# Layer 0's modulation: shift and scale ahead by fp32 products, the other 32 column tiles inside the attention

## The chip, the cores and the metric

The kernel runs on one core of a Trainium2 chip. The metric is the device time of one execution in microseconds (us). Three runs of the kernel before gave 3951.24, 3951.5 and 3957.62 us; the median is 3951.5.

## What is computed

One inference step of a diffusion backbone of four layers. Two groups of tokens run through it, 512 latent tokens and 128 context tokens, each token 1024 wide. Layers 0 and 3 mix tokens by latent attention with 16 heads, layer 1 by an RWKV-7 scan in both directions, layer 2 by pooling; behind each mixer stands a SwiGLU feed-forward block. Each layer gets six vectors per group out of the conditioning, and they steer both its halves:

```
def adaln(cond, w, b):
    m = (jax.nn.silu(cond) @ w + b)[..., None, :]
    return jnp.split(m, 6, axis=-1)

def modulate(x, shift, scale):
    return x * (1.0 + scale) + shift
...
        mp = adaln(c_ctx, ada_w[layer], ada_b[layer])
        ms = adaln(c, ada_w[layer], ada_b[layer])
        hp = modulate(yp, mp[0], mp[1])
        hs = modulate(ys, ms[0], ms[1])
...
        yp = layer_norm(ALPHA * yp + mp[2] * op, ln_g[layer, 0], ln_b[layer, 0])
        ys = layer_norm(ALPHA * ys + ms[2] * os_, ln_g[layer, 0], ln_b[layer, 0])
        fp = swiglu(modulate(yp, mp[3], mp[4]), ffn_wg[layer], ffn_wu[layer], ffn_wd[layer])
```

`ada_w` of a layer is 1024 x 6144 in fp32, 24 MB. The mixer's input needs only the first two of the six vectors (shift and scale, 2048 columns); the gate comes into play behind the mixer's output projection, the last three in the feed-forward block.

## The kernel before

Activations lie transposed in SBUF: `x` is 128 partitions x 8 tiles x 640 tokens. Most products are made three times in fp32r on a high and a low part of both operands (`w_hi`, `w_lo`, `hhi`, `hlo`). The weights come as a stream of 512 KB chunks of eight 128x128 tiles: SP loads them into three raw buffers (`w_raw`), POOL splits them into high and low, and TensorE (PE) takes them in the order of the stream. `panel` (L807, its products at L819) makes one output tile of 128x640 out of eight tiles.

The order of work on each engine is that of the code; the engines meet at semaphores, and at the ends of some stages (`end`) all three of PE, ACT and DVE wait for each other.

**The opening.** SP issues the constants, x (2560 KB) and then layer 0's `ada_w` in 24 units of 1 MB (128 partitions x 4 row tiles x 512 columns) into a ring of four slots. `ada` on ACT (L1523) casts each unit to its high part, on DVE (L2112) subtracts for the low part, and on PE (L825) multiplies: the conditioning (two columns, `silu_hi` and `silu_lo`) is the stationary operand, 512 columns of the unit move (L837). The results are rows of 2x512; ACT copies them out (L1534), and 48 small fp32 products with the identity turn them into columns (L842: two moving columns, a 2x128 stationary operand). DVE copies all 48 tiles out, adds the bias and prepares the combined scales of the layer (`modulation`, L2123). Then ACT modulates x tile by tile and casts (`split_h`, L1546, operations at L1560 and L1552), DVE subtracts (L2169), and PE starts its first panel.

**The attention of layer 0** (`mla`, PE L981, ACT L1617, DVE L2339). Behind the projections eight pairs of heads run in a loop, which PE has unrolled four times. A pair begins with two key panels (L1046) and six query tiles (L819), and then takes ten steps `u`, five blocks of 128 queries for each head. In a step PE makes the scores of block u+1 (`scores`: four fp32 passes of 320 columns at L1067, or two of 128 at L1064 for the context block), turns the exponentials of block u (`turn`: five transposes at L1077) and multiplies those of block u-1 with the values (`av`: five fp32 products of 64 columns, ten passes, at L1091). DVE takes the maximum (L2390), copies the turned tile out (L2413, L2414) and scales the result (`tail`, L2382); ACT makes the exponential (L1682). At a pair's end PE turns the output (L1105). An fp32 product is two passes through PE, so it has two MATMUL and two LDWEIGHTS rows in the trace. After the eighth pair comes the output projection (`out_proj`), whose results DVE multiplies with the gate and adds to x (`gated`, L2181).

Of the kernel before, what the change touches and what calls it, by code (L numbers as in the profile page):

```python
# [49 lines left out]
ADA_SLOTS, ADA_SPLITS = 4, 3  # L50
# [169 lines left out]
def build(nc, a, o):  # L220
    ctx = ExitStack()
    with ctx:
# [19 lines left out]
        sc_hi, sc_lo = sb("silu_hi", [P, KD, 2], F32R), sb("silu_lo", [P, KD, 2], F32R)  # L242
# [28 lines left out]
        stage_free = sem("stage_free")  # L271
        s_init, s_const = sem("s_init"), sem("s_const")
        ada_land = [sem(f"ada_land{i}") for i in range(ADA_SLOTS)]
        unit_land = [sem(f"unit_land{i}") for i in range(2)]
        unit_used, unit_sum, unit_col = sem("unit_used"), sem("unit_sum"), sem("unit_col")
        ada_mm, ada_row, ada_hi, ada_lo = sem("ada_mm"), sem("ada_row"), sem("ada_hi"), sem("ada_lo")
# [12 lines left out]
        def f_ada(m, g):  # L289
            m.rows = g("ada_rows", [2, 6 * D])  # L290
            m.hi, m.lo = ([g(f"ada_{n}{i}", [P, 4, 512], F32R) for i in range(ADA_SPLITS)] for n in ("hi", "lo"))
            m.ring = [g(f"ada_ring{i}", [P, 4, 512]) for i in range(ADA_SLOTS)]
# [19 lines left out]
        def f_mla(L):  # L312
            def f(m, g):
# [20 lines left out]
                m.mx = g(f"m_mx{L}", [P, 2])  # L334
            return f
# [144 lines left out]
        def _(sp):  # L480
            sp.dma_start(cst[:, :], a["cst"]).then_inc(s_const, 16)
            sp.dma_start(x[:, :, :], a["x"].rearrange("k p t -> p k t")).then_inc(s_const, 16)
            done = 0
# [318 lines left out]
        def _(pe):  # L802
# [22 lines left out]
            def ada():  # L825

                m = m_ada
                for cb in range(12):
                    if cb >= 2:
                        pe.wait_ge(ada_row, cb - 1)  # L830
                    for kh in range(2):
                        unit = 2 * cb + kh
                        pe.wait_ge(ada_lo, unit + 1)
                        hi, lo = m.hi[unit % ADA_SPLITS], m.lo[unit % ADA_SPLITS]
                        for n, (w, r) in enumerate(((sc_hi, hi), (sc_lo, hi), (sc_hi, lo))):
                            for k in range(4):
                                last = mm(ps[0:2, 4 + cb % 2, :], w[:, 4 * kh + k, :], r[:, k, :],  # L837
                                          start=kh == 0 and n == 0 and k == 0, stop=kh == 1 and n == 2 and k == 3)
                        last.then_inc(ada_mm, 1)
                pe.wait_ge(ada_row, 12)  # L840
                for n in range(48):
                    mm(ps[:, 6, 2 * n:2 * n + 2], m.rows[0:2, n * P:(n + 1) * P], ident[0:2, 0:2], start=True, stop=True)  # L842
                end()
                end()
# [136 lines left out]
            def mla(L):  # L981
# [526 lines left out]
            pe.wait_ge(s_const, 32)  # L1508
            end()
# [8 lines left out]
        def _(act):  # L1518
# [3 lines left out]

            def ada():  # L1523
                m = m_ada
                for u in range(ADA_UNITS + 3):
                    if u < ADA_UNITS:
                        act.wait_ge(ada_land[u % ADA_SLOTS], 16 * (u // ADA_SLOTS + 1))
                        if u >= ADA_SPLITS:
                            act.wait_ge(ada_mm, u - ADA_SPLITS + 1)
                        nc.scalar.copy(m.hi[u % ADA_SPLITS][:, :, :], m.ring[u % ADA_SLOTS][:, :, :]).then_inc(ada_hi, 1)  # L1530
                    if u >= 4 and u % 2 == 0:
                        cb = u // 2 - 2
                        act.wait_ge(ada_mm, 2 * cb + 2)
                        nc.scalar.copy(m.rows[0:2, cb * 512:(cb + 1) * 512], ps[0:2, 4 + cb % 2, :]).then_inc(ada_row, 1)  # L1534
                end()
                end()
# [80 lines left out]
            def mla(L):  # L1617
# [5 lines left out]
                else:  # L1623
                    split_h(2 * L, x, lambda kt, cd: (mods[0][:, KD + kt, cd:cd + 1], mods[0][:, kt, cd:cd + 1]), m.t32, m.hhi)
# [47 lines left out]
                end()  # L1672
                with act.Fori(0, HEADS // 2) as j:
# [416 lines left out]
            act.wait_ge(s_const, 32)  # L2090
            act.wait_ge(s_init, 2)
            ch(af(sc_c[:, :, :], cond, ACT.Silu))
            nc.scalar.copy(sc_hi[:, :, :], sc_c[:, :, :]).then_inc(s_init, 1)
            end()
            for L in range(DEPTH):
                if L == 0:
                    ada()
# [9 lines left out]
        def _(dve):  # L2107
# [4 lines left out]
            def ada():  # L2112
                m = m_ada
                for u in range(ADA_UNITS):
                    dve.wait_ge(ada_hi, u + 1)
                    tt(m.lo[u % ADA_SPLITS][:, :, :], m.ring[u % ADA_SLOTS][:, :, :], m.hi[u % ADA_SPLITS][:, :, :].bitcast(F32),
                       ALU.subtract).then_inc(ada_lo, 1)
                end()
                ch(cp(mods[0][:, :, :], ps[:, 6, 0:96].rearrange("p (n c) -> p n c", c=2)))
                modulation(0)  # L2120
                end()

            def modulation(L):  # L2123

                mod = mods[L % 2]
                ch(tt(mod[:, :, :], mod[:, :, :], adab[:, L, :].unsqueeze(2).to_broadcast([P, 48, 2]), ALU.add))
                for part in (1, 4):
# [211 lines left out]
            def mla(L):  # L2339
# [28 lines left out]
                with dve.Fori(0, HEADS // 2) as j:  # L2368
# [31 lines left out]
                    copy_pt(dve, q, m, j, 9)  # L2400
                    tail(9)
# [4 lines left out]
                end()  # L2406
                out_proj(L, mods[L % 2][:, 2 * KD:3 * KD, :])
# [372 lines left out]
            nc.vector.memset(eps[:, 3:5], 0.0).then_inc(s_init, 1)  # L2780
            dve.wait_ge(s_const, 32)
            dve.wait_ge(s_init, 3)
            ch(tt(sc_lo[:, :, :], sc_c[:, :, :], sc_hi[:, :, :].bitcast(F32), ALU.subtract))
            end()
# [202 lines left out]
```

## Time and profile before

| | |
|---|---|
| runs of the kernel | 3951.24, 3951.5, 3957.62 us |
| span of the profiled execution | 3955.7 us (its whole time is not listed apart) |
| PE busy | 3625.6 us (92%) |
| PE weight load busy | 3412.5 us (86%) |
| DVE busy | 2466.1 us (62%) |
| ACT busy | 938.1 us (24%) |
| POOL busy | 1840.3 us (47%) |
| chain that ended last | PE 71%, DVE 16% of the span |

The span goes from the first to the last instruction of one profiled execution on the chip. PE is the matmul side of TensorE and PEld its weight loads, which overlap; ends of matmuls are modelled. Busy shares are averages over stages that have different limits. The granted clock is the share of 2.4 GHz that TensorE was given: 1.00 is 2.4 GHz, 0.50 is 1.2 GHz. Where a row ends in brackets, they hold the idle time of the engine before it and what ended that.

### The profile page before, as it was taken

The page shows a single profiled execution, that of the slowest core. Times are in us where ns is not written, and L with a number is a line of the kernel's source. Part 1 is how long each engine was busy: PE and PEld are TensorE (multiplying, and loading weights), DVE is VectorE, ACT ScalarE, POOL GpSimd, SP SyncE. Part 2 cuts the span into 40 slices and gives each one's busy share as a digit, 9 for nine tenths or more (in the row PEclk, how much of TensorE's full clock was granted, in tenths as well). Part 3 has the DMA queues.
Part 4 walks back from the last instruction along what each step waited for, and adds up shares of the span by engine and source line. Part 5 has one row for each costly group of instructions (what it writes and reads, how often), then busy time and mean ns, then how long its engine had stood idle before and what let it go on. Part 6 is the DMA issues. An engine that isn't in the chain of part 4 may idle for free.

```text
span 3955.7 us, 74569 instructions
## 1 busy us (share of the span) xinstructions
PE 3625.6 (92%) x31532; PEld 3412.5 (86%) x31532; DVE 2466.1 (62%) x3517; ACT 938.1 (24%) x1804; POOL 1840.3 (47%) x875
## 2 busy tenths in 40 slices
PE   8999999999889778888999994899999989999998
PEld 3877799999788678888999994799998777899997
DVE  5366678758785466655885768886676566632125
ACT  5322231001244255532310012310013222220011
POOL 1311156665455646535566552466554101356663
PEclk9999999999999888889999997899999999999999
DMA  8200024333235543322343331243332000122221
GB/s 318 62 12 17 17 81 147 136 112 123 70 127 182 149 87 94 84 55 102 114 142 119 124 101 36 90 145 128 123 102 73 27 12 17 43 70 75 76 76 53
DMA packets 226844, 367.60 MB, mean 93 GB/s; under 512 B 104752, under 2 KB 111088, under 8 KB 226416
## 3 DMA queue, kind: packets, MB, share of 16 engines
q1 hardware_dynamic: 171408, 255.08, 20.9%
q10 hardware_dynamic: 55136, 107.98, 7.9%
q8 instruction: 254, 4.16, 0.4%
q14 instruction: 46, 0.38, 0.0%
HBM read 326.47 MB, written 36.54 MB: 92 GB/s over the span
## 4 chain that ended last, share of the span: by engine, by line
PE 71%; DVE 16%; issue 3%; ACT 3%; DMA 1%; SPq 1%; POOL 1%; ACTq 1%; DVEq 0%; POOLq 0%
PE ps L819 52%; PE ps L1091 3%; PE ps L1067 3%; DVE f_acc L2159 2%; PE ps L862 2%; PE ps L1077 2%; DVE m_mx L2390 1%; PE ps L1046 1%; DVE r_t L2456 1%; DVE x L2257 1%; DVE r_hlo L2440 1%; DVE ps L2605 1%; PE ps L1027 1%; DVE x L2266 1%; PE ps L879 1%
## 5 line engine op out<-in xcount | busy, mean ns | idle before, releaser
L674 POOL TENSOR_TENSOR w_hi<-w_raw,zrow 128x1024 fp32r<-128x1024 f32 x354 | 693.7, 1959 | 1783.6 <-PE ps L819 979.9
L676 POOL TENSOR_TENSOR w_lo<-w_raw,w_hi 128x1024 fp32r<-128x1024 f32 x354 | 900.2, 2543 | 27.8
L2159 DVE SCALAR_TENSOR_TENSOR f_acc<-f_unit,silu_c,f_acc 128x512 f32<-128x512 f32 x504 | 631.3, 1293 | 7.6
L819 PE MATMUL ps<-f_hhi,w_hi 128*128 128x320 f32 x2688 | 634.1, 317 | 0.0
L819 PE MATMUL ps<-f_hhi,w_lo 128*128 128x320 f32 x2688 | 613.0, 309 | 0.0
L819 PE MATMUL ps<-f_hlo,w_hi 128*128 128x320 f32 x2688 | 610.8, 308 | 0.0
L819 PEld LDWEIGHTS ps<-f_hlo,w_hi 128*128 128x128 f32 x2688 | 449.6, 188 | 0.0
L819 PEld LDWEIGHTS ps<-f_hhi,w_lo 128*128 128x128 f32 x2688 | 448.9, 188 | 0.0
L819 PEld LDWEIGHTS ps<-f_hhi,w_hi 128*128 128x128 f32 x2688 | 441.2, 188 | 0.0
L819 PE MATMUL ps<-f_ahi,w_hi 128*128 128x320 f32 x1408 | 322.2, 310 | 0.2 <-DVE f_alo L2304 0.2
L819 PE MATMUL ps<-f_alo,w_hi 128*128 128x320 f32 x1408 | 320.9, 309 | 0.0
L819 PE MATMUL ps<-f_ahi,w_lo 128*128 128x320 f32 x1408 | 320.6, 309 | 0.0
L2302 DVE TENSOR_TENSOR f_a<-f_sil,ps 128x640 f32<-128x640 f32 x88 | 72.2, 821 | 376.0 <-ACT f_sil L1603 376.0
L2181 DVE SCALAR_TENSOR_TENSOR x<-ps,mod,x 128x320 f32<-128x320 f32 (+2 forms) x264 | 99.7, 433 | 331.6 <-PE ps L819 330.4
L2304 DVE TENSOR_TENSOR f_alo<-f_a,f_ahi 128x640 fp32r<-128x640 f32 x88 | 201.7, 2293 | 69.9 <-ACT f_ahi L1605 69.9
L819 PEld LDWEIGHTS ps<-f_ahi,w_hi 128*128 128x128 f32 x1408 | 235.6, 188 | 1.1 <-DVE f_alo L2304 0.5
L819 PEld LDWEIGHTS ps<-f_ahi,w_lo 128*128 128x128 f32 x1408 | 235.5, 188 | 0.0
L819 PEld LDWEIGHTS ps<-f_alo,w_hi 128*128 128x128 f32 x1408 | 235.2, 188 | 0.0
L1603 ACT ACTIVATE f_sil<-ps 128x640 f32<-128x640 f32 x88 | 62.3, 708 | 711.7 <-DVE f_acc L2159 383.2
L1091 PE MATMUL ps<-m_V,m_PT 128*128 x1344 | 170.4, 271 | 15.5 <-DVE m_PT L2416 11.7
L1091 PEld LDWEIGHTS ps<-m_V,m_PT 128*128 128x128 f32 x1344 | 162.5, 192 | 22.2 <-issue 20.2
L1682 ACT ACTIVATE m_P<-ps,m_nm 128x640 f32<-128x640 f32 x128 | 101.6, 793 | 332.6 <-DVE m_nm L2394 332.6
(401 smaller groups left out, 6710.4 us busy)
## 6 DMA issues: line engine op xcount, KB each, us to landing
w_raw<-in_w SPq DMA_DIRECT2D x340, 512.0 KB, 3.5
f_unit<-in_ada_w ACTq DMA_DIRECT2D x72, 1024.0 KB, 5.8
ada_ring<-in_ada_w SPq DMA_DIRECT2D x24, 1024.0 KB, 6.6
up_scratch<-r_o ACTq DMA_DIRECT2D x40, 320.0 KB, 3.3
s_LW<-up_scratch SPq DMA_DIRECT2D x16, 320.0 KB, 5.1
s_LA<-up_scratch SPq DMA_DIRECT2D x8, 640.0 KB, 6.6
x<-in_x SPq DMA_DIRECT2D x1, 2560.0 KB, 9.4
x_scratch<-r_o ACTq DMA_DIRECT2D x8, 320.0 KB, 2.2
```

The source lines that it names most:

```text
L674: nc.gpsimd.tensor_tensor(whi[:, slot, :], raw[:, raw_slot, :], zrow[:, 0:1].to_broadcast([P, CH * P]), ALU.add).then_inc(w_hi_done, 1)
L676: nc.gpsimd.tensor_tensor(wlo[:, slot, :], raw[:, raw_slot, :], whi[:, slot, :].bitcast(F32), ALU.subtract).then_inc(w_split, 1)
L819: last = mm(ps[:, 2 * b + h, 0:HT], w, r[:, h * HT:(h + 1) * HT], start=kt == 0 and n < 2, stop=kt == KT - 1 and n >= 4)
L862: last = mm(ps[:, 2 * b + h, 0:HT], w, r[:, h * HT:(h + 1) * HT], start=kt == 0 and n == 0, stop=kt == KT - 1 and n == 2)
L1067: last = mm(ps[:, b + h, 0:HT], m.Q[:, hh, qt * P:(qt + 1) * P], m.K[:, hh, h * HT:(h + 1) * HT], start=True, stop=True)
L1077: last = nc.tensor.transpose(ps[:, 4 + kb // 4, (kb % 4) * P:(kb % 4 + 1) * P], m.pr[:, u % 2, kb * P:(kb + 1) * P], ident)
L1091: last = mm(ps[:, 6, 0:64], m.pt[:, u % 2, kb * P:(kb + 1) * P], m.V[:, kt, bass.ds(j * P + hh * 64, 64)], start=kb == 0, stop=kb == nk - 1)
L1682: af(halves(m.pr[:, u % 2, :]), ps[:, b:b + 2, 0:HT], ACT.Exp, bias=m.nm[:, 2 * (u % 2), 0:1], scale=SM_SCALE, accum_out=m.nm[:, 2 * (u % ...
L2159: last = stt(acc[:, cd, :], unit[:, k, :], by, acc[:, cd, :], ALU.mult, ALU.add)
L2181: last = stt(xs, ps[:, 2 * b + h, t0:t1], gate[:, c, cd:cd + 1], xs, ALU.mult, ALU.add)
L2302: tt(halves(m.a32[:, f % 2, :]), halves(m.sil[:, f % 2, :]), pair(2 * b + 1), ALU.mult).then_inc(q.act, 1)
L2304: tt(m.alo[:, u, :], m.a32[:, f % 2, :], m.ahi[:, u, :].bitcast(F32), ALU.subtract).then_inc(q.lo, 1)
```

## The change

Layer 0's 48 column tiles of modulation are computed in two parts, both on PE in fp32 without a split: a 128x128 tile of `ada_w` is the stationary operand, and the two columns of the conditioning move. A tile takes eight such products and comes out as a column.

- Ahead: the first 16 tiles (shift and scale), out of 8 units in 8 buffers, without a ring. DVE adds the bias out of PSUM and 1 to the scale. ACT's casts, DVE's subtractions, the rows and the turning products are gone, as are three of the common stage ends.
- Inside the attention: the other 32 tiles, four to each pair of heads, in steps u = 1, 3, 6 and 8, between `scores` and `turn` on PE. Each tile is a load of its own (128 partitions x 8 x 128, 512 KB in pieces of 512 bytes) that ACT issues: three at the start of a pair, the fourth in step 3, when the first has been used. DVE copies four tiles out of PSUM at the end of each pair. The rest of `modulation` follows after the attention.
- On SP x is loaded behind the units and the first chunk of weights; the silu waits for the constants alone.

```diff
-ADA_SLOTS, ADA_SPLITS = 4, 3
+EARLY = 2 * KD // 4
+LATE_AT = 2 * KD
+LATE_GROUPS = 4
+LATE_BUFFER = (0, 1, 2, 0)
+LATE_TURN, LATE_AV = (1, 3, 6, 8), ()
...
-            sp.dma_start(x[:, :, :], a["x"].rearrange("k p t -> p k t")).then_inc(s_const, 16)
...
-            for u in range(ADA_UNITS):
-                slot = u % ADA_SLOTS
-                if u >= ADA_SLOTS:
-                    sp.wait_ge(ada_lo, u - ADA_SLOTS + 1)
-                sp.dma_start(m_ada.ring[slot][:, :, :],
+            for u in range(2 * EARLY):
+                sp.dma_start(m_ada.unit[u][:, :, :],
                              src[:, 4 * (u % 2):4 * (u % 2) + 4, (u // 2) * 512:(u // 2 + 1) * 512]
-                             ).then_inc(ada_land[slot], 16)
+                             ).then_inc(ada_land[u // 2], 16)
...
-                    pieces(LAYER_BASE[L], [[(c, 0, CH)] for c in MLA_IN])
+                    order = [[(c, 0, CH)] for c in MLA_IN]
+                    pieces(LAYER_BASE[L], order, 0, 1)
+                    if L == 0:
+                        sp.dma_start(x[:, :, :], a["x"].rearrange("k p t -> p k t")).then_inc(s_x, 16)
+                    pieces(LAYER_BASE[L], order, 1)
...
+                pe.wait_ge(s_cond, 1)
+                for cb in range(EARLY):
+                    units = m_ada.unit[2 * cb:2 * cb + 2]
+                    pe.wait_ge(ada_land[cb], 32)
+                    for n in range(4):
+                        for k in range(KD):
+                            last = mm(ps[:, 6, 8 * cb + 2 * n:8 * cb + 2 * n + 2], units[k // 4][:, k % 4, n * P:(n + 1) * P],
+                                      sc_c[:, k, :], start=k == 0, stop=k == KD - 1)
+                last.then_inc(ada_mm, 1)
+
+            def late(j, p):
+
+                b = LATE_BUFFER[p]
+                pe.wait_ge(ada_land[b], j * 32 + 16 * (p // 3 + 3) if b == 0 else j * 16 + 48)
+                for k in range(KD):
+                    last = mm(ps[:, 7, 2 * p:2 * p + 2], m_mla[0].late[b][:, k, :], sc_c[:, k, :], start=k == 0, stop=k == KD - 1)
+                last.then_inc(late_mm, 1)
...
                         if u < 9:
                             scores(u + 1)
+                        if L == 0 and u in LATE_TURN:
+                            late(j, LATE_TURN.index(u))
                         if u < 10:
                             turn(u)
+                        if L == 0 and u in LATE_AV:
+                            late(j, len(LATE_TURN) + LATE_AV.index(u))
                         if u:
                             av(u - 1)
...
                 else:
+                    act.wait_ge(s_x, 16)
+                    act.wait_ge(ada_mod, 1)
                     split_h(2 * L, x, lambda kt, cd: (mods[0][:, KD + kt, cd:cd + 1], mods[0][:, kt, cd:cd + 1]), m.t32, m.hhi)
...
                 with act.Fori(0, HEADS // 2) as j:
+                    if L == 0:
+                        for p in (0, 1, 2):
+                            load_late(j, p)
                     for u in range(10):
                         qt = u % 5
+                        if L == 0 and u == LATE_TURN[0] + 2:
+                            act.wait_ge(late_mm, j * LATE_GROUPS + 1)
+                            load_late(j, 3)
                         act.wait_ge(q.nmax, q.at.nmax + j * 10 + (u + 1))
...
+                dve.wait_ge(ada_mm, 1)
+                mod = mods[0]
+                ch(tt(mod[:, 0:LATE_AT, :], ps[:, 6, 0:2 * LATE_AT].rearrange("p (n c) -> p n c", c=2),
+                      adab[:, 0, 0:LATE_AT].unsqueeze(2).to_broadcast([P, LATE_AT, 2]), ALU.add))
+                s = mod[:, KD:2 * KD, :]
+                ts(s, s, 1.0, None, ALU.add).then_inc(ada_mod, 1)
...
                     copy_pt(dve, q, m, j, 9)
+                    if L == 0:
+                        dve.wait_ge(late_mm, j * LATE_GROUPS + LATE_GROUPS)
+                        cp(mods[0][:, bass.ds(j * LATE_GROUPS + LATE_AT, LATE_GROUPS), :],
+                           ps[:, 7, 0:2 * LATE_GROUPS].rearrange("p (n c) -> p n c", c=2))
                     tail(9)
...
                 end()
+                if L == 0:
+                    modulation(0)
                 out_proj(L, mods[L % 2][:, 2 * KD:3 * KD, :])
```

On PE the program of before opens with 72 such rows of wide products (three to a unit, the first five here), then the 48 turning products, then the first panel (x4 counts equal products in a row; `m_hhi` is the split x):

```order
L837 MATMUL ps<-ada_hi,silu_hi 2x512 x4
L837 MATMUL ps<-ada_hi,silu_lo 2x512 x4
L837 MATMUL ps<-ada_lo,silu_hi 2x512 x4
L837 MATMUL ps<-ada_hi,silu_hi 2x512 x4
L837 MATMUL ps<-ada_hi,silu_lo 2x512 x4
```

With the change it opens like this (`ada_unit` is the tile of `ada_w`, `silu_c` the conditioning, and L821 the panel's line):

```order
L835 MATMUL ps<-silu_c,ada_unit 128x2 x128
L821 MATMUL ps<-m_hhi,w_hi 128x320 x2
L821 MATMUL ps<-m_hhi,w_lo 128x320 x2
L821 MATMUL ps<-m_hlo,w_hi 128x320 x2
```

All products of 512 columns are gone, and what is left ahead of the first panel is one row of 128 products with two columns.

On SP the queue of before opens so:

```order
L481 DMA cst<-in_cst 128x844
L482 DMA x<-in_x 128x8x640
L648 DMA ada_ring<-in_ada_w 128x4x512 x24
L511 DMA w_raw<-in_w 128x1024 x6
```

and now so:

```order
L484 DMA cst<-in_cst 128x844
L646 DMA ada_unit<-in_ada_w 128x4x512 x8
L512 DMA w_raw<-in_w 128x1024
L659 DMA x<-in_x 128x8x640
L512 DMA w_raw<-in_w 128x1024 x5
```

x has moved behind the units and a chunk of weights, and 16 of the 24 units have left the queue.

In the attention PE's program of before reads so from the value products of step 2 on (`m_K` and `m_Q` make the scores, `cst` and `m_P` the transposes, `m_V` and `m_PT` the value products):

```order
L1091 MATMUL ps<-m_V,m_PT 128x64 x5
L1064 MATMUL ps<-m_K,m_Q 128x128
L1073 REGISTER_ALU
L1077 MATMUL ps<-cst,m_P 128x128 x5
L1091 MATMUL ps<-m_V,m_PT 128x64 x5
L1067 MATMUL ps<-m_K,m_Q 128x320 x2
```

and with the change:

```order
L1092 MATMUL ps<-m_V,m_PT 128x64 x5
L1065 MATMUL ps<-m_K,m_Q 128x128
L842 ISA
L844 MATMUL ps<-silu_c,m_late 128x2 x8
L1074 REGISTER_ALU
L1078 MATMUL ps<-cst,m_P 128x128 x5
L1092 MATMUL ps<-m_V,m_PT 128x64 x5
L1068 MATMUL ps<-m_K,m_Q 128x320 x2
```

A wait (L842) for the tile's load and its eight products have come between the scores and the transposes; the same stands in steps 1, 6 and 8.

## Rows read from the trace of the kernel before

**Rows 1.** The page's slices: granted clock and DMA, 40 equal slices.
```profile
PEclk9999999999999888889999997899999999999999
DMA  8200024333235543322343331243332000122221
```

**Rows 2.** Order of time, opening: start us, length us, engine, line, [idle before <- releaser].
```profile
1.20 0.42 SPq L482 DMA_DIRECT2D x<-in_x  x1
...
10.66 0.22 ACT L2092 ACTIVATE silu_c<-cst 128x16 f32<-128x16 f32 x1 [8.33 <-DMA x<-in_x]
...
13.43 1.90 ACT L1530 CAST ada_hi<-ada_ring 128x2048 fp32r<-128x2048 f32 x1 [2.31 <-DMA ada_ring<-in_ada_w]
...
16.07 1.90 ACT L1530 CAST ada_hi<-ada_ring 128x2048 fp32r<-128x2048 f32 x1 [0.75 <-DMA ada_ring<-in_ada_w]
```

**Rows 3.** The chain that ended last, around the first split: start us, us, what.
```profile
106.89 0.27 DVE mod L2126
...
107.39 0.18 DVE mod L2129
...
108.24 1.21 ACT m_t L1560 x2
...
124.12 22.27 PE ps L819 x150
```

**Rows 4.** Order of time, PE in the first pair of heads and its end.
```profile
184.71 0.61 PE L1046 MATMUL ps<-m_khi,w_hi 128*128 128x384 f32 x2 [1.01 <-ACTq L473]
...
197.84 1.23 PE L1091 MATMUL ps<-m_V,m_PT 128*128 x10
...
200.58 1.23 PE L1091 MATMUL ps<-m_V,m_PT 128*128 x10
...
220.30 0.59 PE L1046 MATMUL ps<-m_khi,w_hi 128*128 128x384 f32 x2
```

**Rows 5.** Waits of PE, 189 to 431 us: total us, times, longest us.
```profile
PE ps L1077 <- ACT m_P L1682: 6.9, 13, 0.8
PE ps L1091 <- DVE m_PT L2416: 4.4, 6, 0.7
...
PE ps L1105 <- DVE m_O L2382: 2.7, 6, 0.5
```

**Rows 6.** L842 in two windows (busy us and count, granted clock), then durations, min/median/max ns.
```profile
88.60:92.00 3.40, 3.37 (x29) 3.37 (x29) 0.95 0.36 135
92.00:104.00 12.00, 12.00 (x58) 12.00 (x58) 0.50 0.43 132
...
L842 PEld LDWEIGHTS ps<-cst,ada_rows x96: 181/328/328, 88.6 to 106.1; 2*128 2x128 f32 x96
...
L879 PEld LDWEIGHTS ps<-cst,f_acc x576: 187/188/192, 625.0 to 2961.9; 128*128 128x128 f32 x192
```

**Rows 7.** Windows: length, busy and count of PE, PEld, DVE, ACT, POOL; clock; DMA.
```profile
112.00:116.00 4.00, 4.00 (x17) 3.51 (x15) 1.85 (x3) 3.94 (x8) 0.00 (x0) 0.56 0.00 0
...
196.00:212.00 16.00, 15.69 (x105) 12.89 (x104) 12.24 (x38) 5.44 (x14) 0.00 (x0) 1.00 0.00 1
...
252.00:256.00 4.00, 2.58 (x17) 2.15 (x18) 1.12 (x5) 0.00 (x0) 0.00 (x0) 0.94 0.00 0
256.00:258.00 2.00, 2.00 (x9) 2.00 (x8) 0.57 (x1) 1.29 (x3) 1.03 (x1) 0.50 0.03 8
258.00:260.00 2.00, 2.00 (x11) 2.00 (x10) 0.49 (x3) 0.74 (x1) 1.92 (x2) 0.77 0.00 0
```

**Rows 8.** Order of time, four rows of ACT and DVE; then the page's DMA issues.
```profile
230.06 0.79 ACT L1682 ACTIVATE m_P<-ps,m_nm 128x640 f32<-128x640 f32 x1 [7.33 <-DVE m_nm L2394]
...
482.98 7.19 DVE L2174 TENSOR_SCALAR x<-x 128x640 f32<-128x640 f32 x8
...
492.52 1.13 DVE L2181 SCALAR_TENSOR_TENSOR x<-ps,mod,x 128x320 f32<-128x320 f32 x3 [2.34 <-PE ps L819]
...
611.82 0.37 ACTq L1543 DMA_DIRECT2D f_unit<-in_ada_w  x1
...
f_unit<-in_ada_w ACTq DMA_DIRECT2D x72, 1024.0 KB, 5.8
```

More of the change, by code:

```diff
@@ L270, in build @@
         stage_end = sem("stage_end")
-        stage_free = sem("stage_free")
-        s_init, s_const = sem("s_init"), sem("s_const")
-        ada_land = [sem(f"ada_land{i}") for i in range(ADA_SLOTS)]
+        s_init, s_const, s_x, s_cond, s_eps = sem("s_init"), sem("s_const"), sem("s_x"), sem("s_cond"), sem("s_eps")
+        ada_land = [sem(f"ada_land{i}") for i in range(EARLY)]
         unit_land = [sem(f"unit_land{i}") for i in range(2)]
         unit_used, unit_sum, unit_col = sem("unit_used"), sem("unit_sum"), sem("unit_col")
-        ada_mm, ada_row, ada_hi, ada_lo = sem("ada_mm"), sem("ada_row"), sem("ada_hi"), sem("ada_lo")
+        ada_mm, ada_mod, late_mm = sem("ada_mm"), sem("ada_mod"), sem("late_mm")
         outs_done = sem("outs_done")
@@ L289, in f_ada @@
         def f_ada(m, g):
-            m.rows = g("ada_rows", [2, 6 * D])
-            m.hi, m.lo = ([g(f"ada_{n}{i}", [P, 4, 512], F32R) for i in range(ADA_SPLITS)] for n in ("hi", "lo"))
-            m.ring = [g(f"ada_ring{i}", [P, 4, 512]) for i in range(ADA_SLOTS)]
+            m.unit = [g(f"ada_unit{i}", [P, 4, 512]) for i in range(2 * EARLY)]
         def f_ffn(L):
@@ L334, in f @@
                 m.mx = g(f"m_mx{L}", [P, 2])
+                if L == 0:
+                    spare = m.t32.rearrange("p a t -> p (a t)")[:, 0:KD * P].rearrange("p (k n) -> p k n", k=KD)
+                    m.late = [g(f"m_late{b}", [P, KD, P])[:, :, :] for b in range(2)] + [spare]
             return f
@@ L825, in ada @@
             def ada():
[L827 to L844, printed above, removed]
+                pe.wait_ge(s_cond, 1)
[13 more added lines that the diff above has]
+                last.then_inc(late_mm, 1)
             def twins(KT, hi, lo, pairs, ready, highs):
@@ L1521, in _ @@
             af = nc.scalar.activation
[L1523 to L1536, printed above, removed]
             def load_unit(L, h):
@@ L1672, in mla, with load_late @@
                 end()
+                late_src = a["ada_w"][0].rearrange("(k p) n -> p k n", p=P)
+                def load_late(j, p):
+                    act.dma_start(m.late[LATE_BUFFER[p]], late_src[:, :, bass.ds(j * (LATE_GROUPS * P) + (LATE_AT + p) * P, P)]
+                                  ).then_inc(ada_land[LATE_BUFFER[p]], 16)
                 with act.Fori(0, HEADS // 2) as j:
+                    if L == 0:
+                        for p in (0, 1, 2):
+                            load_late(j, p)
                     for u in range(10):
                         qt = u % 5
+                        if L == 0 and u == LATE_TURN[0] + 2:
+                            act.wait_ge(late_mm, j * LATE_GROUPS + 1)
+                            load_late(j, 3)
                         act.wait_ge(q.nmax, q.at.nmax + j * 10 + (u + 1))
@@ L2087, in pooling @@
                        scale=lna[:, 1, 0, kt:kt + 1]).then_inc(q.xs, 1)
[L2090 to L2094, printed above, removed]
+            act.wait_ge(s_const, 16)
+            act.wait_ge(s_eps, 1)
+            af(sc_c[:, :, :], cond, ACT.Silu).then_inc(s_cond, 1)
             for L in range(DEPTH):
-                if L == 0:
-                    ada()
                 (mla, rwkv, pooling)[MIXER[L]](L)
@@ L2112, in ada @@
             def ada():
[L2113 to L2121, printed above, removed]
+                dve.wait_ge(ada_mm, 1)
[4 more added lines that the diff above has]
+                ts(s, s, 1.0, None, ALU.add).then_inc(ada_mod, 1)
             def modulation(L):
                 mod = mods[L % 2]
-                ch(tt(mod[:, :, :], mod[:, :, :], adab[:, L, :].unsqueeze(2).to_broadcast([P, 48, 2]), ALU.add))
-                for part in (1, 4):
+                n0 = 0 if L else LATE_AT
+                ch(tt(mod[:, n0:48, :], mod[:, n0:48, :], adab[:, L, n0:48].unsqueeze(2).to_broadcast([P, 48 - n0, 2]), ALU.add))
+                for part in (1, 4) if L else (4,):
                     s = mod[:, part * KD:(part + 1) * KD, :]
@@ L2779, in _ @@
             nc.vector.memset(eps[:, 2:3], GN_EPS)
[L2780 to L2784, printed above, removed]
+            nc.vector.memset(eps[:, 3:5], 0.0).then_inc(s_eps, 1)
             for L in range(DEPTH):
```

5 lines of the change are left out of this document (1 added, 4 removed).

## Prediction, made before the changed kernel ran

> **What bounds the kernel now.** I read the slices first, then the opening in order of time, then the chain of waits, then the windows with the granted clock, and last the attention of layer 0 by groups, in order of time and by waits. The slices [rows 1] show DMA full in the first of 40 slices and nearly idle in slices 3 to 5, where layer 0's attention stands: the change moves load from the first place to the second. The opening [rows 2] shows ACT taking a 1 MB unit every 2.7 us (13.43, 16.07), after x landed at 10.66. All 24 units must have passed before the chain [rows 3] reaches the split of x at 108.24; PE's first panel is paced by that split until 124.12. So whatever brings 108.24 forward brings the whole end forward one for one. In the attention TensorE bounds: a step of five transposes, ten value passes and four score passes goes from 197.84 to the same place in the next step in about 2.75 us without a gap, and one pair of heads from 184.71 to 220.30 in 35.6 us [rows 4], while its longest kinds of waits for ACT and DVE sum to 14.0 us in 242 us (6.8 pairs), near 2.1 us a pair [rows 5].
>
> **Part 1, the opening.** Removed: 24 casts, 24 subtractions, 288 wide products and the 48 turning products (96 passes), 16 of the 24 units, and the wait of the silu for x. Added: 128 fp32 products, two passes each, 256 passes with two moving columns on 128x128 weights. When they start: the first unit was cast at 13.43 behind x (2560 KB, some 6.6 us at 2.7 us a MB), so it is there at 6.8 and the second at 9.5. What a pass costs: L842 is the same kind, fp32 with two moving columns. At the full clock 29 passes take 3.4 us, and L842's passes in 92 to 104, at clock 0.50, are 58 in 12.00 us [rows 6]: 0.11 and 0.21 us. The weight load of a full 128x128 tile with one moving column (L879) lasts 188 ns, that of L842 at its shortest 181 [rows 6], so 128 rows cost no more than 2. Which level? L842 began at 1.00 behind a dense stretch, kept PE busy without a gap, and the clock fell to 0.50 some 3 us after its first pass and stayed there until the panels, 112 to 116 [rows 6, 7]. The new products begin after idleness and are of that kind alone, so I take the 1.2 GHz level throughout: 256 x 0.21 = 54, ending at 63.5. The last result, DVE's add (0.26) and +1 (0.18) and two handovers are 0.8: split of x at 64.3 in place of 108.24, a gain of 43.9 us. By the same 2.7 us a MB the 8 units are there by 26, the first chunk of weights and x behind them by 34; with POOL's splits of the first chunks all this lies under PE. Were the passes all at the full level, 256 x 0.11 = 28, the split would start near 38.5 and the gain be 70; that is the other bound.
>
> By the Trainium skill ("TensorE: Matmul & The Clock Gate", Part 1) what halves the clock is TensorE's idleness, and activity releases it; the new products leave it no idleness, so by that rule the gain would be the 70. The trace disagrees for just this kind of product: PE busy 12.00 of 12.00 us at 0.50 [rows 6].
>
> **Part 2, the late products.** 32 column tiles, four to a pair of heads, each 8 products or 16 passes: 64 passes a pair. At the full clock 64 x 0.112 = 7.2 us a pair. They stand between scores and transposes, where PE sometimes waits for the exponential: those waits are 6.9 us in 6.8 pairs, 1.0 a pair [rows 5], and a little more goes on the weight side; I take 1.2 as cover. Left 6.0 us a pair, 48 us over eight. With no cover it is 57.
>
> **Part 3, what they do to the clock.** In before, nearly every fall in this attention comes at a pair's end, where PE has only transposes and 64-column value passes and no scores: 0.94 in 252 to 256, 0.50 in 256 to 258, 0.77 in 258 to 260, back only after the next pair's panels have run [rows 7]. That stretch is like the one made here four times a pair: 1.8 us of two-column passes, followed by 0.6 us of transposes and 1.1 us of value passes. At two of the four places (third and eighth step) even the scores ahead are the short ones, 2 passes in place of 4. And in the middle of a pair there are no panels to bring the clock back. Lower bound: no fall, 0. Upper bound: half clock from the first group to the end of the pair, 197 to 220 and 7.2 us of new passes, some 28 us of passes that take twice as long: less some 1 us of cover +27 a pair, 216 in all. I take the row nearest to it, a fall that lasts about 4 us [rows 7], once for each group: 16 us a pair at half speed, 8 us lost, less 1.3 us of waits for ACT and DVE that a slower PE no longer meets: 6.7 us a pair, 54 in all. From two falls a pair (2.7 net) to five or six (10.5 net) it is 22 to 84. That a group brings about one fall is my choice: the stretch in the rows is the nearest in kind, and no row shows the new one itself.
>
> **Part 4, edits at nothing.** ACT issues four loads a pair, 0.37 us each; three stand at the pair's start, where ACT waits 7.33 us for the first maximum, and the fourth before the fourth exponential, while PE has a late group before the transposes that need it. Without cover it is 0.4 x 8 = 3 us. The 512 KB tiles have 10 us until their use; a unit twice as large lands in 5.8 [rows 8]. The queue ahead is idle [rows 1]. Behind PE's wait for a late tile stand the transposes and all the rest, so a late landing would be paid in full. DVE's copy of 128x8 stands before the last tail, which waits for PE. The rest of the modulation, about five small operations of 0.2 us [rows 3], now stands ahead of scaling x (482.98, 7.19 us); the first gated update then waits 2.34 us for PE [rows 8]: 1.1 us is hidden there.
>
> **Sum.** -43.9 + 48 + 54 = +58 us on a span of 3955.7, so 4013.8. The profiled execution's span lies 4.2 us above the median of the runs, 3951.5, so the median I expect is 4009.6: 4010 us.
>
> **Rivals.**
> A, the clock holds in the attention but not in the opening: -43.9 + 48 = +4, 3955.6. For it: most of each step is still scores, transposes and value passes, and 16 us of before with those stand at 1.00 [rows 7]. Against: [rows 7].
> B, the other side, faster: 128-row weight loads count as work for the clock, so both places run at 2.4 GHz: -70 + 48 = -22, 3930. L842 loads weights of only two rows, so the trace leaves this open. Against it: the passes at the ends of pairs load full 128x128 tiles (18 in 4 us) and the clock falls [rows 7]. It decides if the opening's passes run at 0.11 soon after their start.
> C, a late tile isn't there when PE asks: three loads of 512 KB in short rows on one queue. If each pair waits 3 us for one, +24 on top of the forecast: 4034. Against: DMA idle there.
> D, the change gives back the opening but the falls last to each pair's end: about +216 in place of 54, 4171. Against: a stretch with scores stays at 1.00 in before, and at half clock scores fill PE's time again, which may raise it before the panels come.
>
> **How the numbers follow.** The forecast with its own spread (3976 to 4040: falls 22 to 84, weaker cover) 0.70, A 0.12, B 0.09, C 0.05, D 0.04. 0.2% of 3951.5 is 7.9 us, about what a measurement of this kernel can tell from no change. Faster by more needs B: 0.09 and 0.01 of A. Same takes 0.08 of A. Slower is the rest, 0.82. The range reaches down to A, 3952, and up to 4045 with C inside: B, D and a sliver of the forecast stay out, 0.17. The likeliest case's own range is 3976 to 4040.
>
> **What would show each step.** Right: PE's opening passes 0.21 us apart at clock 0.50, first panel product near 68, a granted clock well under 0.9 in the attention, with 0.50 inside pairs, pairs of 43 to 52 us, late groups of 1.8 us at the one level and 3.4 at the other, the attention some 100 us longer. Wrong: opening passes at 0.11 (B), pairs of 41 to 42 us at clock 0.95 (A), PE idle before a late group (C), pairs over 60 (D). All stages behind the attention should keep their lengths within a few us.

## The result and the profile after

| | before | changed |
|---|---|---|
| median of four runs | 3951.37 us (3947.86 to 3957.62) | 3996.8 us (3987.25 to 4008.99) |
| ratio | 1 | 1.0114, 95% interval 1.0092 to 1.0136 |
| span of the profiled execution | 3955.7 us | 3991.2 us (its run: 3992.98) |
| first split of x starts | 108.24 | 64.87 |
| attention of layer 0, first key panel to output projection | 184.7 to 483.1: 298.4 us | 141.3 to 525.8: 384.4 us |
| behind the attention | 3472.6 us | 3465.4 us |

The change is slower by 45 us; 58 were forecast. In the spans: -43.4 in the opening, +86.0 in the attention, -7.2 behind it, together +35.5. I read the same views in the same order as before the run. First the changed kernel's page: its slices and two groups of DMA issues (KB each, median us to landing).

```profile
PEclk9978899999989979988999997899999999999999
DMA  4212113434225544323343331244332000122221
...
m_late<-in_ada_w ACTq DMA_DIRECT2D x24, 512.0 KB, 4.0
...
m_t<-in_ada_w ACTq DMA_DIRECT2D x8, 512.0 KB, 6.4
```

DMA is no longer full in the first slice and stays light in the next ones [rows 1], and the late tiles land in 4.0 and 6.4 us, within the 10 us that they have. The clock reads 7 to 8 in slices 3 to 5, where most of the attention stands. Next the chain that ended last (start us, us, what), and L835's rows by duration (min/median/max ns, first and last start).

```profile
1.67 7.79 DMA ada_unit<-in_ada_w
...
9.60 54.76 PE ps L835 x256
...
64.87 1.21 ACT m_t L1548 x2
```
```profile
L835 PEld LDWEIGHTS ps<-silu_c,ada_unit x256: 286/333/333, 9.6 to 63.9; 128*128 128x128 f32 x128
L835 PE MATMUL ps<-silu_c,ada_unit x256: 342/352/352, 9.6 to 64.0; 128*128 128x2 f32 x128
```

256 passes in 54.76 us are 0.214 us each, and no weight load was shorter than 286 ns, where one at the full level lasts 188 [rows 6]. So all of them ran at the 1.2 GHz level. There is a trap here: the granted clock of this stretch reads 1.00, as the first row below shows, because the clock's record holds only changes, and its first entry in this trace, a rise, comes at 72.6. Before it, the level has to be read from the durations of weight loads.

Windows of the changed kernel: the opening, the first and second pair of heads, the whole attention, then four stretches inside the second pair and two around its end at 236.5; the columns are those of [rows 7]. The last row is the attention of the kernel before.

```profile
20.00:60.00 40.00, 40.00 (x189) 40.00 (x189) 0.00 (x0) 0.00 (x0) 16.86 (x8) 1.00 0.55 206
...
141.30:184.40 43.10, 40.93 (x280) 36.89 (x280) 22.58 (x63) 9.29 (x21) 7.75 (x4) 0.93 0.26 74
184.40:236.50 52.10, 49.75 (x282) 44.31 (x280) 23.84 (x65) 10.04 (x23) 4.27 (x2) 0.76 0.18 51
141.30:525.70 384.40, 361.61 (x2232) 324.02 (x2232) 188.27 (x521) 81.28 (x185) 37.71 (x18) 0.84 0.20 57
...
198.70:202.00 3.30, 3.30 (x32) 3.25 (x30) 1.87 (x6) 0.89 (x2) 0.00 (x0) 1.00 0.03 8
202.00:206.50 4.50, 4.50 (x22) 3.66 (x22) 2.41 (x8) 0.89 (x2) 0.00 (x0) 0.62 0.39 111
206.80:209.00 2.20, 2.20 (x23) 2.20 (x22) 0.67 (x3) 0.46 (x2) 0.00 (x0) 1.00 0.00 0
209.00:220.30 11.30, 11.30 (x43) 9.28 (x41) 4.89 (x15) 1.77 (x4) 0.00 (x0) 0.55 0.01 1
...
229.60:236.50 6.90, 5.39 (x25) 4.75 (x24) 1.78 (x9) 0.00 (x0) 0.00 (x0) 0.50 0.00 0
236.50:239.90 3.40, 3.40 (x13) 3.40 (x12) 0.89 (x2) 0.93 (x3) 2.59 (x2) 0.50 0.36 90
```
```profile
184.70:483.00 298.30, 271.45 (x1720) 231.94 (x1720) 184.78 (x513) 81.06 (x185) 37.75 (x18) 0.96 0.05 17
```

And PE in order of time in that second pair, around two of its late groups (start us, length us):

```profile
198.74 1.84 PE L844 MATMUL ps<-silu_c,m_late 128*128 128x2 f32 x16
...
202.09 2.20 PE L1068 MATMUL ps<-m_K,m_Q 128*128 128x320 f32 x4
204.09 1.27 PE L1078 MATMUL ps<-cst,m_P 128*128 128x128 f32 x5
...
206.78 1.84 PE L844 MATMUL ps<-silu_c,m_late 128*128 128x2 f32 x16
...
211.00 2.45 PE L1068 MATMUL ps<-m_K,m_Q 128*128 128x320 f32 x4
...
223.74 1.29 PE L1068 MATMUL ps<-m_K,m_Q 128*128 128x320 f32 x4
```

A late group (the eight products of one late tile) costs 1.84 us itself and runs at the full level, as all 32 do. The price comes behind it: the four score passes, 1.29 us at the full level (223.74), take 2.20 and 2.45, and the stretch behind the second group stands at 0.55 for 11.3 us. PE was busy in all of the first four stretches (11.30 of 11.30 in the last of them), so it is not idleness that goes with these falls.

The clock's record places the falls. All 17 begin 1.9 to 3.6 us after the start of a late group. The first three groups of a pair bring a fall in 9 of 24 cases, of 4.6 us on average. The fourth group brings one in all eight pairs; it lasts 10.2 us or more, over the pair's end into the panels behind it (229.6 to 239.9 above), and up to the pair's end PE does idle for 1.5 us. Together these eight hold 84 of the 125 us at the low level. In the kernel before, the six falls stand at pairs' ends.

Pairs last 43.1, 52.1, 48.9, 48.8, 45.6, 52.2, 45.8 and 48.0 us, where they were 35.6 to 40.6.

PE's waits from 145 to 435 us of the changed kernel (total us, times, longest us) are no longer than those of [rows 5], and none of them is for a late tile:

```profile
PE ps L1078 <- ACT m_P L1685: 5.0, 6, 0.8
PE ps L1092 <- DVE m_PT L2420: 4.4, 6, 0.7
PE ps L1110 <- DVE m_O L2380: 2.7, 6, 0.5
```

### The profile page after: what moved, and what is told of

It is laid out like the page before. It is cut to its first block, busy times and chain, and to the rows that moved or that the text cites. A ratio compares the mean times of both kernels' runs of the same rounds, so it can differ in the third digit from the quotient of the medians.

```text
span 3991.2 us, 75370 instructions
## 1 busy us (share of the span) xinstructions
PE 3683.7 (92%) x31916; PEld 3518.6 (88%) x31916; DVE 2414.0 (60%) x3500; ACT 886.9 (22%) x1767; POOL 1837.4 (46%) x875
## 4 chain that ended last, share of the span: by engine, by line
PE 80%; DVE 12%; issue 3%; ACT 2%; DMA 1%; SPq 1%; POOL 1%; ACTq 0%; DVEq 0%; POOLq 0%
PE ps L821 56%; PE ps L1092 4%; PE ps L1068 3%; PE ps L863 2%; PE ps L1078 2%; PE ps L835 1%; PE ps L844 1%; PE ps L1047 1%; DVE r_t L2460 1%; DVE r_hlo L2444 1%; PE ps L880 1%; DVE x L2255 1%; DVE m_mx L2388 1%; DVE ps L2609 1%; PE ps L1028 1%
## 5 line engine op out<-in xcount | busy, mean ns | idle before, releaser
L821 PE MATMUL ps<-f_hhi,w_hi 128*128 128x320 f32 x2688 | 634.0, 317 | 0.0
L821 PE MATMUL ps<-f_hhi,w_lo 128*128 128x320 f32 x2688 | 613.2, 309 | 0.0
L821 PE MATMUL ps<-f_hlo,w_hi 128*128 128x320 f32 x2688 | 610.7, 308 | 0.0
L821 PEld LDWEIGHTS ps<-f_hlo,w_hi 128*128 128x128 f32 x2688 | 449.8, 188 | 0.0
L821 PEld LDWEIGHTS ps<-f_hhi,w_lo 128*128 128x128 f32 x2688 | 448.8, 188 | 0.0
L821 PEld LDWEIGHTS ps<-f_hhi,w_hi 128*128 128x128 f32 x2688 | 441.1, 188 | 0.0
L821 PE MATMUL ps<-f_ahi,w_hi 128*128 128x320 f32 x1408 | 321.8, 310 | 0.0
L821 PE MATMUL ps<-f_ahi,w_lo 128*128 128x320 f32 x1408 | 320.9, 309 | 0.0
L821 PE MATMUL ps<-f_alo,w_hi 128*128 128x320 f32 x1408 | 320.8, 309 | 0.0
L821 PEld LDWEIGHTS ps<-f_ahi,w_hi 128*128 128x128 f32 x1408 | 235.5, 188 | 0.6
L821 PEld LDWEIGHTS ps<-f_alo,w_hi 128*128 128x128 f32 x1408 | 235.5, 188 | 0.0
L821 PEld LDWEIGHTS ps<-f_ahi,w_lo 128*128 128x128 f32 x1408 | 235.2, 188 | 0.0
L1092 PE MATMUL ps<-m_V,m_PT 128*128 x1344 | 190.9, 291 | 15.5 <-DVE m_PT L2420 11.7
L1092 PEld LDWEIGHTS ps<-m_V,m_PT 128*128 128x128 f32 x1344 | 182.6, 211 | 24.4 <-issue 23.0
```

The lines of the kernel that those rows point to most:

```text
L821: last = mm(ps[:, 2 * b + h, 0:HT], w, r[:, h * HT:(h + 1) * HT], start=kt == 0 and n < 2, stop=kt == KT - 1 and n >= 4)
L1092: last = mm(ps[:, 6, 0:64], m.pt[:, u % 2, kb * P:(kb + 1) * P], m.V[:, kt, bass.ds(j * P + hh * 64, 64)], start=kb == 0, stop=kb == nk - 1)
```

## The experiments

Theory: late products cost their own passes, about 48 us, and further time because a stretch of two-column passes takes TensorE's clock down behind it, about 38 us. Rival 1: the second part is contention or waits, for the late loads, ACT's issues or DVE. Rival 2: the clock falls whatever the passes move. All kernels start from the changed one. In the table, "low" is the time in the attention that the clock's record shows at the 1.2 GHz level, with the number of falls. Each ratio is to runs of the kernel before that were made beside it (medians 3951.03 to 3953.59). The stages are those of one profiled execution of each kernel; times in us.

| kernel | median | ratio to before (95%) | split of x | attention | low (falls) | behind |
|---|---|---|---|---|---|---|
| before, profiled once | 3951.37 | 1 | 108.2 | 298.4 | 23 (6) | 3472.6 |
| changed | 3996.8 | 1.0114 (1.0092 to 1.0136) | 64.9 | 384.4 | 125 (17) | 3465.4 |
| e8, changed again | 4000.96 | 1.0134 (1.0108 to 1.016) | 65.0 | 382.4 | 121 (17) | 3466.2 |
| e1, no late tiles | 3903.86 | 0.9884 (0.9866 to 0.9902) | 64.8 | 297.9 | 23 (6) | 3462.6 |
| e6, one product in eight | 3913.64 | 0.9897 (0.9878 to 0.9915) | 65.1 | 302.7 | 33 (6) | 3468.9 |
| e2, late ones wide | 3957.02 | 1.0017 (1.0007 to 1.0027) | 64.9 | 340.4 | 13 (3) | 3465.6 |
| e3, opening wide | 3982.87 | 1.0076 (1.0059 to 1.0092) | 42.8 | 396.4 | 150 (21) | 3468.5 |
| e4, both wide | 3938.22 | 0.9966 (0.9953 to 0.998) | 42.9 | 350.7 | 39 (7) | 3466.7 |
| e5, halves | 3956.34 | 1.0002 (0.999 to 1.0013) | 65.0 | 344.3 | 42 (8) | 3466.9 |
| e9, steps 0, 3, 6, 10 | 3961.57 | 1.0022 (1.0011 to 1.0034) | 65.0 | 354.6 | 76 (17) | 3467.3 |
| e7, both wide, those steps | 3917.51 | 0.9908 (0.9891 to 0.9925) | 42.5 | 327.2 | 3 (1) | 3469.1 |
| e10, e7 with a warm start | 3914.79 | 0.9904 (0.9886 to 0.9923) | 40.8 | 327.1 | 3 (1) | 3468.3 |
| e11, e7 again | 3915.16 | 0.9905 (0.9887 to 0.9923) | 40.7 | 326.6 | 4 (2) | 3467.8 |

**Without the late tiles (e1).** The calls of `late` on PE, of `load_late` on ACT and the copy on DVE go, and DVE sets those parts of the modulation to zero; its core:

```diff
-                        if L == 0 and u in LATE_TURN:
-                            late(j, LATE_TURN.index(u))
...
-                        for p in (0, 1, 2):
-                            load_late(j, p)
```

> Leaves out the 32 late column tiles: their loads, products and copies (those parts of the modulation are zero). The opening is as changed. Clock theory: the attention of layer 0 is back at the 298 us and the clock of before, and only the opening's 43.4 us remain: 3951 - 43 = 3908 us, some 88 below the changed kernel's 3997. Rival, that x and the units now share the queue with the weight stream and the projections pay for it: the stages behind the split are longer than before and the time is above 3920.

Measured: 3903.86, 4 us below the expectation, with the attention and its clock back to those of before. Windows, and waits of PE from 145 to 435 us (total us, times, longest us), both of e1:

```profile
141.30:439.00 297.70, 271.22 (x1720) 231.75 (x1720) 184.89 (x512) 80.95 (x185) 37.70 (x18) 0.96 0.05 17
```
```profile
PE ps L1078 <- ACT m_P L1675: 8.1, 16, 0.8
PE ps L1092 <- DVE m_PT L2406: 5.1, 7, 0.7
```

So all 86 us hang on what was added per pair, and the opening is worth its 43 us alone.

**Loads without products (e6).** The late tiles are loaded, waited for and copied as in the changed kernel; only `for k in range(KD)` becomes `range(1)`, and the one product closes its sum.

> Leaves out seven of eight products of each late tile (that part of the modulation is then a partial sum); all loads, waits, the issues on ACT and the copies on DVE stay. Clock theory: 8 passes a pair, 0.9 us, most of it in PE's waits: within 5 us of the kernel without late tiles, 3904 to 3909. Rival, loads of 512 KB in 512-byte pieces, their issue on ACT and the added waits hold the attention up: 3915 or more.

Measured: 3913.64, some 5 us above the expectation; the attention is 4.8 us longer than in e1, of which up to 5 can be the clock (33 us at the low level in place of 23), and the rest stands behind it (3468.9 against 3462.6), in a part that varies from kernel to kernel. Loads, issues, waits and copies together with 64 of the 512 passes cost under 5 us. Rival 1 falls.

**The same passes with 128 columns (e2, e3, e4).** The two columns are repeated 64 times as the moving operand; weights, passes and loads stay.

```diff
+            def wide(k):
+
+                return sc_c[:, k, :].unsqueeze(1).to_broadcast([P, P // 2, 2])
...
-                    last = mm(ps[:, 7, 2 * p:2 * p + 2], m_mla[0].late[b][:, k, :], sc_c[:, k, :], start=k == 0, stop=k == KD - 1)
+                    last = mm(ps[:, 7, P * p:P * (p + 1)], m_mla[0].late[b][:, k, :], wide(k), start=k == 0, stop=k == KD - 1)
```

e2 does so for the late tiles, e3 for the opening, e4 for both; DVE reads the first two of each 128 columns.

> The late products move 128 columns (the two columns of the conditioning, repeated 64 times) in place of 2; as many passes on the same weights at the same places. Clock theory: a pass still takes 0.11 us, since it is bound by its weight load, but the clock holds inside the pairs: pairs of 41 to 42 us in place of 43 to 52, attention 346 in place of 384, total near 3957. Rival, the late groups cost what they cost by the weight loads, loads from memory or waits that they add, and the clock is a bystander: no change, 3997, or slower by the longer passes.

> Only the opening's 128 products move 128 columns in place of 2. Clock theory: passes of 0.21 us for the first some 5 us, then 0.11: the split of x starts at 40 to 42 in place of 64.9, total 3997 - 24 = 3973. Rival, the opening's clock is low because TensorE has just woken and stays so whatever moves: no change; or passes of 128 columns take longer than their weight load and the opening gets longer.

> Both places move 128 columns. Clock theory: the sum of the two, opening 24 us shorter and attention 38 shorter: 3997 - 62 = 3935, faster than the kernel before (3951) by 0.4%. Rival: 3997.

The attention of e2, and L839, the opening's passes, in e4:

```profile
141.30:481.00 339.70, 317.23 (x2232) 285.98 (x2232) 186.51 (x519) 80.61 (x185) 37.81 (x18) 0.98 0.23 64
```
```profile
L839 PEld LDWEIGHTS ps<-silu_c,ada_unit x256: 191/191/338, 9.6 to 40.9; 128*128 128x128 f32 x128
L839 PE MATMUL ps<-silu_c,ada_unit x256: 273/273/553, 9.6 to 41.0; 128*128 128x128 f32 x128
```

e2 has as many passes as the changed kernel (x2232), the same loads and the same idle time of PE (339.70 - 317.23 = 22.5 us, against 22.8), and stands at 0.98 in place of 0.84; its attention is 44.0 us shorter. So the clock is the difference. 64 times the columns cost next to nothing: from a group's start to the next product it is 1.79 us in place of 1.71, 2.6 us in all. Inside a pair the clock doesn't fall any more; the three falls left stand at pairs' ends. Rival 2 falls. By the medians the difference is 39.8 us, since the trace of e2 is of the fastest of its ten runs, 7.8 us below their median. In the opening the first loads last up to 338 ns, but the median is 191: with 128 columns the level rises within the passes, and all 256 end at 41 in place of 64. e3 missed its expectation by 10 us: the opening came 22 us earlier as said, but the attention was 12 us longer than in the changed kernel, with 150 us at the low level in place of 125 (its trace is of the slowest of its four runs, 4.9 us above their median). Its late groups were not edited, so how often they bring a fall also hangs on something besides their code; the runs do not tell what.

**Narrow, but spread (e5, e9).** The passes keep their two columns. e5 does each tile as four and four products in steps 1 and 2, 3 and 4, 6 and 7, 8 and 9; e9 has the whole groups at `LATE_TURN = (0, 3, 6, 10)`, so that one stands in the wait for the first exponential and one behind the last transposes.

> The same late products as in the changed kernel, two moving columns, in twice as many pieces: a tile's eight products stand as four and four in steps 1 and 2, 3 and 4, 6 and 7, 8 and 9. Clock theory: what brings the clock down is an unbroken stretch of such passes together with the transposes and value passes behind it; pieces of 0.9 us between full steps bring it down less often: attention near 350 to 365 in place of 384, total 3965 to 3978. Rival, each narrow pass takes its share wherever it stands: no change, 3997.

> The changed kernel with two moving columns in both places, but its late groups in steps 0, 3, 6 and 10. Clock theory: place alone helps little, since each group is still one unbroken stretch of 1.8 us of two-column passes: the clock still falls inside most pairs, low for 80 us or more of the attention; total 3965 to 3985. Rival, that e7 gained by the place and not by the width: attention near 327 as there, total 3940.

Both directions were right. e5 gained more than expected, 9 us beyond its range: its low time fell from 125 to 42 us with not one pass fewer, and its eight falls stand behind the last half of each pair, none earlier in a pair. e9 came out 3 us below its range and took 30 us off the attention, and here the low time is 76 us in as many falls (17) as in the changed kernel. The 50 us less are those of the fourth group alone: put off to step 10, next to the following pair's panels, it still brings a fall in each pair, but in six of eight one of 3.4 us. So place shortens the falls and fills waits; with 354.6 against the 327.2 of e7 below, it does not replace the width.

**The best version (e7, e11), and a warm start (e10).** e7 joins e4 and e9's steps (the fourth load then goes out in step 2); e10 adds twelve fp32 products of constants with 128 columns ahead of the first unit.

```diff
-LATE_TURN, LATE_AV = (1, 3, 6, 8), ()
+LATE_TURN, LATE_AV = (0, 3, 6, 10), ()
```
```diff
+                pe.wait_ge(s_const, 16)
+                for n in range(12):
+                    mm(ps[:, 7, 0:P], ident, ones, start=True, stop=True)
                 pe.wait_ge(s_cond, 1)
```

> Both places move 128 columns, and the late groups stand in steps 0, 3, 6 and 10 (ahead of the last value products) in place of 1, 3, 6 and 8. Theory: PE's waits in a pair (0.84 ahead of the first transposes, 0.73 ahead of the last value passes) cover part of two groups: 1 to 1.4 us less a pair, 3938 - 10 = 3928. Rival: the chain over ACT and DVE gets later by as much, no change: 3938.

> e7 (128 moving columns in both places, late groups in steps 0, 3, 6 and 10), and ahead of the opening's products 12 fp32 products of 128 columns on constants, which TensorE runs while it waits for the first unit. Clock theory: the opening's passes run at 0.11 us from the first on and end near 38 in place of 41: 3 us less than e7. Rival, the clock rises no earlier or x and the units are the bound by then: no change.

> e7 once more, beside e10 on the same chip and with five rounds: 3917 again, faster than the kernel before by 0.9%.

The attention of e7, its waits of PE from 123 to 410 us, and PE at the start of a pair and at its end:

```profile
119.90:447.00 327.10, 315.20 (x2232) 283.95 (x2232) 186.66 (x521) 81.24 (x185) 37.74 (x18) 0.99 0.23 67
```
```profile
PE ps L1051 <- issue: 3.4, 1, 3.4
PE ps L1114 <- DVE m_O L2384: 3.1, 7, 0.5
PE ps L1096 <- DVE m_O L2384: 1.6, 7, 0.2
```
```profile
169.57 1.95 PE L848 MATMUL ps<-silu_c,m_late 128*128 128x128 f32 x16
171.36 0.71 PE L1082 MATMUL ps<-cst,m_P 128*128 128x128 f32 x5
...
195.55 1.30 PE L1096 MATMUL ps<-m_V,m_PT 128*128 x10 [0.23 <-DVE m_O L2384]
196.69 2.00 PE L848 MATMUL ps<-silu_c,m_late 128*128 128x128 f32 x16
198.53 0.33 PE L1096 MATMUL ps<-m_V,m_PT 128*128 x2
```

PE's waits for the exponential and for the turned copy are gone: the late group stands in both places. The attention costs 29 us more than without late tiles, for 57 us of passes; up to 10 us of this gap are the clock (3 us low in place of 23). e7 came out 10 us under its expectation, since the clock held there as well. It ran twice, at 0.9908 and 0.9905: about 0.95% below the kernel before, and some 2% below the changed one. PE's passes in e10:

```profile
4.04 5.49 PE L835 MATMUL ps<-cst 128*128 128x128 f32 x24 [4.04 <-DMA cst<-in_cst]
9.88 29.00 PE L842 MATMUL ps<-silu_c,ada_unit 128*128 128x128 f32 x256 [0.35 <-DMA ada_unit<-in_ada_w]
```

The opening's passes now take 0.113 us from the first on and end at 38.9, where they end at 41.1 in e7 and at 40.0 in e11, but the first split starts at 40.8, as in e11 (40.7), and the medians of the two agree. The last section shows what took the gain.

**The changed kernel again (e8).** No edit.

> The changed kernel once more, beside the other three on the same chip: 3997 again, with pairs of 43 to 52 us.

4000.96 us, and an attention of 382.4: the result repeats on another occasion. The falls are 17 again, eight of them behind the fourth groups and with 87 of the 121 us, but the others stand behind other groups than in the first trace of the same code. The first pair shows it, with four falls, 50.6 us and 0.79 where there was one, 43.1 us and 0.93:

```profile
141.40:192.00 50.60, 48.23 (x280) 42.86 (x280) 22.91 (x63) 9.28 (x21) 7.75 (x4) 0.79 0.22 63
```

## Why the prediction was right, point by point

- **The opening, -43.9:** measured -43.4. The first unit was waited for until 9.60, where I had 9.5; 256 passes took 54.76 us, forecast 54. Taking the 1.2 GHz level throughout was right. What would show it was named wrongly: the record reads 1.00 there. The first panel product came at 67.74, forecast near 68.
- **The late products, +48:** e2 less e1 is 42.5 us in the traces. e2 stood 10 us less at the low level than e1, worth up to 5 us, so the passes themselves are between 42 and 48 (by the medians e2 less e1 is 53.2, since e2's trace is a fast one). The cover of 1.2 us a pair was about right in size, but only 0.5 of it are waits: PE's idle time falls from 26.5 us in e1 to 22.5 in e2. Where the rest is hidden was not shown.
- **The clock, +54:** the changed kernel less e2 is 44.0 (39.8 by the medians); less those up to 5 us it is 39 to 44. This is the term that was mis-sized. I had said one fall of 4 us for each group, 32 falls and 128 us more at half speed. Measured are 17 falls in place of 6 and 103 us more at the low level. The two kinds of group differ. For the first three of a pair the length was about right (4.6 us), but only 9 of 24 brought a fall. The fourth always did, and its fall lasted 10.2 us or more. So there are fewer falls than forecast and longer ones, and the two errors partly cancel: that part of the agreement is luck. The 1.3 us of spared waits a pair are not seen either, since PE idles 22.8 us in the changed kernel and 22.5 in e2.
- **A row read wrongly:** I read [rows 7] as a clock that is back only after the next pair's panels have run, and argued from it that nothing brings it back in the middle of a pair. In the trace of before it fell at 255.5 and was back at 258.9, 2.7 us into panels that run from 256.2 to 264.9, and in the changed kernel it is back at 219.4 with no panel near:

```profile
258.90:264.90 6.00, 6.00 (x41) 6.00 (x41) 2.73 (x3) 0.00 (x0) 2.40 (x1) 1.00 0.29 87
```

- **Edits at nothing:** right within 5 us (e6), DVE's copies included. The modulation's rest stands in e1 too, so no experiment leaves it out, but the trace shows it hidden: it takes 1.05 us on DVE ahead of scaling x (525.64 to 526.69), and the first gated update behind it still waits 1.30 us for PE, where it waited 2.34 [rows 8]:

```profile
535.07 1.14 DVE L2179 SCALAR_TENSOR_TENSOR x<-ps,mod,x 128x320 f32<-128x320 f32 x3 [1.30 <-PE ps L821]
```

- **Behind the attention, no change:** measured -7.2. The twelve other profiled executions of the table lie between 3462.6 and 3469.1, whatever was edited, and only that of the kernel before lies at 3472.6; the run in which it was profiled was also the slowest of its four (3957.62, median 3951.37). That it is the spread between executions is my reading; with one trace of before it stays open.
- **The total, 4010 for 3996.8:** it is closer than the terms are. In the spans 4013.8 were forecast and 3991.2 measured, 22.6 less: some 16 in the attention and 7.2 behind it. Of this 9.8 came back by chance, because the profiled execution of before lies 4.2 us above the median and that of the changed kernel 5.6 below its own.
- **The rivals.** A, the clock holds in the attention: refuted, pairs of 43 to 52 us at 0.84. e2 is what A would look like, at 3957.02 (A: 3955.6). B, weight loads of 128 rows hold the clock: refuted by the opening, 256 such loads at the low level; e4 differs from it only in the columns moved and in where PSUM takes them. C, a late tile comes too late: refuted, the waits of PE above hold none for a load, and e6 is cheap. D, falls to each pair's end: true of the fourth group alone. A fall behind the second group lasts from 209.2 to 219.4, but the scores at 223.74, in the same pair, run at the full level again, and a price of 39 to 44 us is far from D's 216.

By the Trainium skill ("TensorE: Matmul & The Clock Gate", Part 1) activity releases the throttle and idleness brings it back. For passes that move two columns the runs do not agree: 54.76 us without a gap stayed at the low level. With 128 columns (e4) they agree. In which measure activity is counted is not told by these runs.

## What to carry to other kernels

Moving a vector product from a DMA-bound opening onto TensorE is cheap to count in passes and can still cost as much again in the clock; price the stretch behind the added passes, not only the passes. Where narrow products stand between wide ones, let them move more columns if that leaves the pass's duration as it is, and put them where the engine waits. And before the first entry of the clock's record, read the level from the durations of weight loads.

## What the runs showed of the hardware that was not expected

A pass of fp32 with 2 and one with 128 moving columns take nearly the same 0.11 us at the full level (16 in 1.84 us and in 1.95, L844 and L848 above); so the wide form is almost free.

DVE and POOL slow each other where their work meets. In e4 the split of x begins at 42.85, while POOL is still splitting chunks of weights until 50.49; the last two of POOL's operations take 2.47 and 2.83 us, and the two before them 1.89 and 2.34. DVE's rows there, in order of time:

```profile
41.58 1.17 DVE L2122 TENSOR_SCALAR mod<-mod 128x16 f32<-128x16 f32 x1
...
48.55 3.35 DVE L2171 TENSOR_TENSOR m_hlo<-m_t,m_hhi 128x640 fp32r<-128x640 f32 x2 [0.30 <-ACT m_hhi L1544]
...
53.20 0.82 DVE L2171 TENSOR_TENSOR m_hlo<-m_t,m_hhi 128x640 fp32r<-128x640 f32 x1 [1.29 <-ACT m_hhi L1544]
```

The small operation takes 0.18 us in [rows 3] and 1.17 here; two subtractions take 3.35 us beside POOL and 0.82 each behind it. In e10 the same small operation lasts 1.53 us from 39.15, where it lasts 0.34 in e11. This 1.2 us takes back what the warm start had gained on e11's passes (38.9 against 40.0):

```profile
38.31 2.34 POOL L678 TENSOR_TENSOR w_lo<-w_raw,w_hi 128x1024 fp32r<-128x1024 f32 x1
39.15 1.53 DVE L2125 TENSOR_SCALAR mod<-mod 128x16 f32<-128x16 f32 x1
40.61 1.89 POOL L676 TENSOR_TENSOR w_hi<-w_raw,zrow 128x1024 fp32r<-128x1024 f32 x1
```

DVE's operation ends when POOL's does (38.31 + 2.34 is 40.65, 39.15 + 1.53 is 40.68), and so it does in e4, e7 and e11, where it lasts 1.17, 1.03 and 0.34 us and ends 0.02 to 0.03 us behind POOL's. The Trainium skill ("SBUF — State Buffer", "SBUF: two separate sides") says that the two share a pair of ports as an exclusive lock, held for a whole instruction. The waiting for POOL's end agrees with it; whether an operation with one small input falls under the page's condition (a 2-port mode, or two inputs from SBUF) these rows do not tell.

The changed kernel's runs spread over 22 us, where the four of the kernel before spread over 10. This goes with falls that come behind some groups and not behind others, and the two traces of the same code (changed and e8) show that they differ from run to run. That they make the whole spread was not shown.
